# Strassen feed-forward: convolution borders on ScalarE, the convolution in one stretch, weight splits in pairs, another order on VectorE, token sums without GpSimd

## The chip, the cores and the metric

One core of one Trainium2 chip runs the whole program. The metric is the time of one execution in device microseconds (us), the median over several runs. Engines are named PE (TensorE, matrix products), ACT (ScalarE), DVE (VectorE), POOL (GpSimd) and SP (SyncE, which here only issues DMAs).

## The reference, cut to what matters

The program is one step of an encoder trunk of two layers for two groups of requests with shared weights: a prompt of 16 meta tokens and 512 frames, and 8 sample streams of 16 frames. In each layer a token mixer (attention and a gated recurrence) is followed by a gated feed-forward with a causal convolution of width 3. The change is in the feed-forward, and in its two ends.

```
h = rmsnorm(x, p['norm_ffn_pre'])
u = h @ p['w_ffn_up']                                   # 1024 -> 2 x 2816
a, v = u[..., :D_FF], u[..., D_FF:]
ext = concatenate([buf, a], axis=1)                     # 2 earlier rows ahead of each stream
c = ffn_conv_b + sum(ext[:, j:j + T] * w[j] for j in range(3))
f = (silu(c) * v) @ p['w_ffn_down']                     # 2816 -> 1024
x = x + rmsnorm(f, p['norm_ffn_post'])
new_buf = ext[:, -2:]
```

## The kernel before, in words

**Layout.** Everything is held as features x tokens: 128 features on the partitions, 656 tokens on the free axis (528 of the prompt, then 8 x 16 of the samples). A matrix product works on halves of 328 tokens. Weights and activations are in float32 and are multiplied in three products: each operand is split into a rounded high part and the remainder as the low part. ACT writes the high part (`whi`, `gh`, `Hh`, `Sh`), DVE subtracts it from the original for the low part (`wlo`, `gl`, `Hl`, `Sl`). One 128x128 weight block so costs three matmuls of 128x328 for each half. The helpers that record an instruction give all of an engine's the same line: 768 for PE, 2100 for DVE, 1453 for ACT; the tiles' names tell them apart.

**Up projection.** The 2816 features are 22 chunks of 128 (`KF`), each with an `a` part and a `v` part. The first three (`NPL`) are plain: six tiles, weight pieces P_UP to P_UP+5. Chunks 3 to 21 are computed by Strassen's seven products in the order B11, B21, T2, T3, T1, T4, B22. Each needs a split weight of 128x512 (a *unit*): B11, B21 and B22 are quarters of the loaded pieces, T1 to T4 are sums of them. GpSimd forms the sums by DMAs that add in memory, one after another: `sum_t3`, `sum_t4`, then `sum_t1` and `sum_t2` of the next chunk (lines 725, 733, 711, 719). Each waits for the one before it; T2 lies in `t2` (two buffers), T3 in `t3` (one), and T3's own start is loaded by SP when the last chunk's T3 has been split. T4 is written over B21, and so waits for the split of B21. The products go to banks of `G0`/`G1` and of `WA`. The token side of the products is `Hh`/`Hl` and the sums `Sh`/`Sl`, made once per layer: GpSimd's `token_sums` writes two differences into `Y`, ACT and DVE scale and add them there, `s_high` and `s_low` split them.

**What follows a chunk.** DVE adds products into `ax` (`a`, first half of the tokens after B21, the second after T4, by way of the buffers `p1`, `p7` and `u2`, which ACT fills by copies). The names in the convolution: `halo(c)` copies the two earlier rows of each sample stream from `cout` into `ax`, `carry(c)` copies the last two rows of `a` into `cout`, both on DVE. `conv_first` (ACT) is the first tap with the bias, `conv_rest` (DVE) the other two, each in two pieces: 528 prompt tokens and 8 x 16 sample tokens. `silu` and `g_high` are ACT's, `times_v` and `g_low` DVE's. The convolution of a chunk (the *pending* one) is done while the next chunk's products run.

**Down projection.** The chunks are in groups (0 to 1, 2 to 5, 6 to 9, 10 to 13, 14 to 17, 18 to 21). After each group TensorE multiplies its 4 chunks into 8 output tiles n = 0 to 7 (three banks of PSUM in rotation), and DVE adds them to `Y`; after the first group ACT copies them.

**What sets the order.** Every engine's instructions are written out by hand, with semaphores. Split units stand in a ring of six half slots. `split_after` gives for each unit the place in ACT's and DVE's order at which it is split: when the unit whose slot it takes has been used, later by `LATE` units of its kind. `chunk(c, pending)` calls `lows(l, u)` (DVE) and `highs(l, u)` (ACT), which issue the splits due up to unit `u`.

```
LATE = {B11: 0, B21: 0, T2: 2, T3: 1, T1: 1, T4: 1, B22: 0}
...
            if _k and product_of(_w):
                _w += LATE[_k[1]]
            _i = max(_i, _w)
            split_after.setdefault(_i, []).append(_u)
```

## Time and profile before

| | |
|---|---|
| time, median of 3 runs (range) | 1988.31 us (1988.12 to 1990.95) |
| profiled execution: time, span of its core | 1987.89 us, 1986.1 us |
| granted clock of TensorE, mean | 0.985 |
| PE busy | 1825.2 us (92%) |
| PE weight loads busy | 1658.3 us (83%) |
| DVE busy | 1313.5 us (66%), 2229 instructions |
| ACT busy | 962.6 us (48%), 1601 instructions |
| POOL busy | 242.9 us (12%) |
| chain of waits that ended last | PE 58%, DVE 21%, ACT 10%, DMA 5%, issue 4% |

The profile is of one execution. A row of the views gives a start and a duration in us, the engine, the program's line, and output and input tiles; what stands in brackets is the engine's idle time just before and what ended it. The chain of waits is followed back from the last instruction, at each step to what released it. The granted clock is TensorE's, as a share of its full speed.

### The profile page before, as it was taken

The numbers are of one execution on the slowest core, as the hardware profiler recorded it, in microseconds if no ns is written. First come the engines' busy times: TensorE is split into PE (matmuls) and PEld (weight loads), VectorE is DVE, ScalarE is ACT, GpSimd is POOL, SyncE is SP. The second block draws the span as 40 slices with busy tenths as digits, with TensorE's granted clock in tenths as the row PEclk, the third lists the DMA queues.
The fourth block names the chain that finished last, engine by engine and source line by source line (L and its number), as shares of the span: only waits on it lengthen the run. The fifth ranks groups of instructions, "written<-read, shape, count | busy, mean of one in ns | idle before, by whom it ended". The sixth has DMA issues, their size and how long they took to land.

```text
span 1986.1 us, 31514 instructions
## 1 busy us (share of the span) xinstructions
PE 1825.2 (92%) x11636; PEld 1658.3 (83%) x11636; DVE 1313.5 (66%) x2229; ACT 962.6 (48%) x1601; POOL 242.9 (12%) x261
## 2 busy tenths in 40 slices
...
GB/s 189 72 55 66 68 89 46 131 54 49 152 123 138 144 145 131 133 154 123 43 107 55 52 72 80 63 118 68 65 84 132 133 131 150 131 140 150 139 69 59
DMA packets 98713, 203.71 MB, mean 103 GB/s; under 512 B 16800, under 2 KB 35616, under 8 KB 98536
## 3 DMA queue, kind: packets, MB, share of 16 engines
...
HBM read 170.65 MB, written 8.65 MB: 90 GB/s over the span
## 4 chain that ended last, share of the span: by engine, by line
PE 58%; DVE 21%; ACT 10%; DMA 5%; issue 4%; DVEq 0%; POOL 0%; ACTq 0%; SPq 0%; POOLq 0%
PE G L768 36%; PE WA L768 12%; PE WB L768 8%; DVE tmp L2100 6%; DVE wlo L2100 4%; ACT tmp L1453 3%; DMA t<-in_wstream 3%; DVE ax L2100 2%; DVE Y L2100 2%; DMA wraw<-in_wstream 1%; PE G L772 1%; ACT sq L1453 1%; DVE gl L2100 1%; ACT Y L1453 1%; PE WB L772 1%
## 5 line engine op out<-in xcount | busy, mean ns | idle before, releaser
L768 PE MATMUL G<-Hh,wlo 128*128 128x328 f32 x1384 | 456.8, 330 | 56.5 <-DVE p L2100 32.5
L768 PE MATMUL G<-Hh,whi 128*128 128x328 f32 x1384 | 436.8, 316 | 0.0
L768 PE MATMUL G<-Hl,whi 128*128 128x328 f32 x1384 | 435.8, 315 | 0.0
L768 PEld LDWEIGHTS G<-Hh,wlo 128*128 128x128 f32 x1384 | 264.3, 191 | 76.5 <-DVE p L2100 40.2
L768 PEld LDWEIGHTS G<-Hh,whi 128*128 128x128 f32 x1384 | 264.6, 191 | 2.3 <-issue 0.4
L768 PEld LDWEIGHTS G<-Hl,whi 128*128 128x128 f32 x1384 | 263.8, 191 | 0.0
L1453 ACT ACTIVATE whi<-wraw 128x1024 fp32r<-128x1024 f32 (+2 forms) x194 | 160.3, 826 | 184.2 <-PE G L768 113.2
L2100 DVE TENSOR_TENSOR wlo<-wraw,whi 128x1024 fp32r<-128x1024 f32 (+2 forms) x194 | 181.7, 936 | 45.1 <-ACT whi L1453 28.2
L768 PE MATMUL G<-gh,wlo 128*128 128x328 f32 x424 | 136.1, 321 | 23.5 <-DVE tmp L2100 17.1
L2100 DVE SCALAR_TENSOR_TENSOR tmp<-ax,cols,tmp 128x528 f32<-128x528 f32 (+1 forms) x176 | 98.6, 560 | 57.9 <-ACT tmp L1453 51.8
L768 PE MATMUL G<-gh,whi 128*128 128x328 f32 x424 | 134.5, 317 | 0.0
L768 PE MATMUL G<-gl,whi 128*128 128x328 f32 x424 | 133.3, 314 | 0.0
L768 PE MATMUL G<-Sh,wlo 128*128 128x328 f32 x304 | 97.2, 320 | 25.8 <-DVE wlo L2100 25.8
L2100 DVE TENSOR_TENSOR wlo<-wff,whi 128x512 fp32r<-128x512 f32 (+1 forms) x118 | 91.3, 774 | 27.3 <-ACT whi L1453 16.3
L1453 ACT ACTIVATE whi<-wff 128x512 fp32r<-128x512 f32 (+1 forms) x118 | 82.6, 700 | 50.5 <-PE WB L768 33.0
L768 PEld LDWEIGHTS G<-gh,wlo 128*128 128x128 f32 x424 | 81.1, 191 | 28.0 <-DVE tmp L2100 20.4
L1453 ACT ACTIVATE tmp<-ax,cols 128x528 f32<-128x528 f32 x88 | 58.3, 662 | 88.1 <-DVE cout L2100 85.8
L768 PE MATMUL G<-Sl,whi 128*128 128x328 f32 x304 | 95.0, 313 | 0.0
L1453 ACT ACTIVATE whi<-t 128x512 fp32r<-128x512 f32 x76 | 48.2, 635 | 96.0 <-PE G L768 53.1
L768 PE MATMUL G<-Sh,whi 128*128 128x328 f32 x304 | 94.5, 311 | 0.0
L768 PE MATMUL WA<-Hh,wlo 128*128 128x328 f32 x216 | 70.6, 327 | 20.7 <-ACT p L1453 20.7
L768 PEld LDWEIGHTS G<-Sh,wlo 128*128 128x128 f32 x304 | 57.2, 188 | 32.4 <-issue 32.4
...
## 6 DMA issues: line engine op xcount, KB each, us to landing
...
t<-in_wstream SPq DMA_DIRECT2D x76, 256.0 KB, 4.1
t<-in_wstream POOLq DMA_DIRECT2D x38, 256.0 KB, 5.5
...
wff<-in_wstream POOLq DMA_DIRECT2D x20, 256.0 KB, 4.2
t<-wff POOLq DMA_DIRECT2D x20, 256.0 KB, 3.3
wff<-t POOLq DMA_DIRECT2D x20, 256.0 KB, 3.3
```

The costliest lines, as they stand in the source:

```text
L768: return pe.matmul(out, lhsT, rhs, start=start, stop=stop, skip_group_check=True)
L772: return pe.transpose(out, in_, ident[0:n, 0:n])
L1453: return act.activation(*args, **kw)
L2100: return kind(*args, **kw)
```

## The change

What it does, part by part.

- **Pairs.** Where two units that follow one another lie side by side in the ring and are due together, they are split by one instruction of 1024 columns, not two of 512 (`pair_of`, `w_high_two`, `w_low_two`). `t2` and `t3` become one tile `t23` so that T2 and T3 can be a pair. The due places are set anew by `LATE`.
- **Convolution.** ACT does `halo` and `carry`. The convolution goes into a buffer of its own, `cc`, in one stretch of 672 columns (prompt, and samples with the columns between them), so two instructions on DVE for four and one on ACT for two; `silu` takes the result from `cc` in two pieces. `cc` lies over `cos4`, so that `cos4` is loaded anew in layer 1 (four DMAs on SP).
- **Order.** DVE's `chunk` takes the low parts ahead of the convolution and the pairs at other places; ACT's copies `p7` after `g_high`. Where the feed-forward starts, the plain chunks, weight splits and sums stand in another order.
- **Token sums.** `token_sums` goes from GpSimd. The sums are formed by DVE from `X` (`s_sum`) in `Sf`, `gh_f` and `gl_f`, which lie over `Sh`, `gh` and `gl`; three of the splits into `Sh` and `Hh` now stand in the first down pass, on ACT behind the copy of `Y` for n = 3.
- **Ends.** Behind the last down pass the additions for tiles 3 and 4 stand further back, ACT's table load and the splits of the next layer's first weights further ahead.

The diff, cut to what the text speaks of (the ends are as the last point says):

```diff
-LATE = {B11: 0, B21: 0, T2: 2, T3: 1, T1: 1, T4: 1, B22: 0}
+LATE = {B11: 1, B21: 0, T2: 1, T3: 0, T1: 0, T4: 1, B22: 0}
+PAIRS = (B11, T2, T4)
...
-if not l:
-    sp.dma_start(cos4[32 * i:32 * i + 32, :], a["rope"][64:96, :]).then_inc(S("cos_in"), 16)
+sp.dma_start(cos4[32 * i:32 * i + 32, :], a["rope"][64:96, :]).then_inc(S("cos_in"), 16)
...
-def token_sums(l):
-    pool.wait_ge(S("hl"), (l + 1) * SPLITS)
-    a_, b_ = cols_of(0), cols_of(1)
-    pool.tensor_tensor(Y[:, 0:KH, a_], X[:, 0:KH, a_], X[:, 0:KH, b_], ALU.subtract).then_inc(S("d"), 1)
-    pool.tensor_tensor(Y[:, KH:KD, a_], X[:, KH:KD, b_], X[:, KH:KD, a_], ALU.subtract).then_inc(S("d"), 1)
...
+def pair_of(g):
+    k = product_of(g % UNITS_L)
+    return k is not None and k[1] in PAIRS and ring[g + 1] == ring[g] + 1 and \
+        any(g % UNITS_L in v and g % UNITS_L + 1 in v for v in split_after.values())
...
+def w_high_two(l, u):
...
+act.wait_ge(S(unit_end(w)[0]), unit_end(w)[1])
...
-w_high(l, v)
+if pair_of(l * UNITS_L + v):
+    w_high_two(l, v)
+elif not pair_of(l * UNITS_L + v - 1):
+    w_high(l, v)
...
+def halo(c):
+    step(f(samples(ax[:, c % 2, 2 + PT:EXT], DT + 2)[:, :, 0:2],
+           cout[:, c, 2:2 + DB * 2].rearrange("p (b t) -> p b t", t=2), ACT.Copy))
 def conv_first(c):
-    k = l * KF + c
-    act.wait_ge(S("conv"), 2 * k + 1)
+    act.wait_ge(S("ax"), l * KF + c + 1)
+    did(f(cc[:, 0:EXT - 2], ax[:, c % 2, 0:EXT - 2], ACT.Identity, scale=cols[:, l, C_CW + c:C_CW + c + 1],
+          bias=cols[:, l, C_CB + c:C_CB + c + 1]), "silu")
+def carry(c):
+    step(f(cout[:, c, :].rearrange("p (b t) -> p b t", t=2),
+           samples(ax[:, c % 2, PT - DT:EXT], DT + 2)[:, :, DT:DT + 2], ACT.Copy))
+def silu(c):
+    act.wait_ge(S("conv"), l * KF + c + 1)
+    k, d = l * KF + c, tmp[:, c % 2, :]
     if k >= 2:
         act.wait_ge(S("gl"), 2 * k - 2)
-    s_, d = ax[:, c % 2, :], tmp[:, c % 2, :]
-    kw = dict(scale=cols[:, l, C_CW + c:C_CW + c + 1], bias=cols[:, l, C_CB + c:C_CB + c + 1])
-    step(f(d[:, 0:PT], s_[:, 0:PT], ACT.Identity, **kw))
-    did(f(samples(d[:, PT:T]), samples(s_[:, 2 + PT:EXT], DT + 2)[:, :, 0:DT], ACT.Identity, **kw), "silu")
-def silu(c):
-    act.wait_ge(S("conv"), 2 * (l * KF + c) + 2)
-    did(f(tmp[:, c % 2, :], tmp[:, c % 2, :], ACT.Silu), "silu")
...
+w_high(l, P_UP + 4)
 for k in range(KH):
...
+halo(0)
 conv_first(0)
-act.wait_ge(S("d"), 2 * l + 1)
-for k in range(KH):
-    did(f(Y[:, k, cols_of(0)], Y[:, k, cols_of(0)], ACT.Copy, scale=cols[:, l, C_FFNPRE + k:C_FFNPRE + k + 1]), "s_act")
+halo(1)
+carry(0)
+w_high(l, P_UP + 5)
 silu(0)
-w_high(l, P_UP + 4)
+conv_first(1)
+carry(1)
 g_high(0)
-w_high(l, P_UP + 5)
-conv_first(1)
-s_high(Sh[:, 1, :, :], 4, 0, 1, -1.0)
 silu(1)
 w_high(l, P_UP + 6)
 g_high(1)
-s_high(Sh[:, 2, :, :], 0, 0, 0)
+halo(2)
+conv_first(2)
+carry(2)
+s_high(Sh[:, 1, :, :], Sf[:, 1, :, :], 8, -1.0)
+s_high(Sh[:, 2, :, :], Sf[:, 2, :, :], 4)
+silu(2)
 w_high(l, P_UP + 7)
...
 conv_first(pending)
+carry(pending)
...
+halo(c)
 highs(l, u0 + B21)
 after(T2)
 did(f(u2, bank(G[s], 0), ACT.Copy), "act_took")
 highs(l, u0 + T2)
+if pending is not None:
+    g_high(pending)
 after(T3)
 act.wait_ge(S("gl"), 2 * (l * KF + c) - 1)
 did(f(p7[:, :], bank(WA, s), ACT.Copy), "act_took")
-if pending is not None:
-    g_high(pending)
-highs(l, u0 + T3)
...
-    s_high(Hh[:, 0:KH, cols_of(1)], 8, 1, 0)
 g_high(last_c)
 for n in range(KD):
     if not q:
         act.wait_ge(S("down"), down_no(l, q, n))
-        act.wait_ge(S("s_dve"), s_split(l, 1 if n < KH else 3))
         did(f(two(Y[:, n, :]), halves(down_bank(n)), ACT.Copy), "act_took")
+    if not q and n == 3:
+        s_high(Sh[:, 0, :, :], Sf[:, 0, :, :], 18)
+        act.wait_ge(S("tile"), t0 + T_UP + 2 * NPL)
+        for x in range(2):
+            s_high(Hh[:, 2 * x:2 * x + 2, cols_of(1)], s4_part(x), 12, -1.0)
...
+def w_low_two(l, u):
+    g = l * UNITS_L + u
+    dve.wait_ge(S("w_hi"), g + 2)
+    did(tt_(pair_in(wlo, g), raw_pair(g), pair_in(whi, g), ALU.subtract), "w_split", by=2)
...
 def conv_rest(c):
     dve.wait_ge(S("silu"), 2 * (l * KF + c) + 1)
-    s_, d = ax[:, c % 2, :], tmp[:, c % 2, :]
-    sv, dv = samples(s_[:, 2 + PT:EXT], DT + 2), samples(d[:, PT:T])
+    n_ = EXT - 2
     for i in (1, 2):
-        w = col(l, C_CW + i * KF + c)
-        step(stt(d[:, 0:PT], s_[:, i:i + PT], w, d[:, 0:PT], ALU.mult, ALU.add))
-        did(stt(dv, sv[:, :, i:i + DT], w, dv, ALU.mult, ALU.add), "conv" if i == 2 else "dve")
...
+def s_sum(to, k, x, minus, plus=False):
+    did(stt(to, X[:, k, cols_of(x)], col(l, C_FFNPRE + k), minus, ALU.mult, ALU.add if plus else ALU.subtract),
+        "s_dve")
...
 plain_a(0)
+plain_a(1)
+w_low(l, P_UP + 4)
 conv_rest(0)
-dve.wait_ge(S("s_act"), 2 * KH * l + KH)
+dve.wait_ge(S("s_act"), S_ACT * l + KH)
 for k in range(KH):
...
 plain_v(1)
+plain_a(2)
 w_low(l, P_UP + 6)
 g_low(1)
+conv_rest(2)
+plain_v(2)
+w_low(l, P_UP + 7)
...
+    s_sum(s4_part(k // 2)[:, k % 2, :], KH + k, 0, Sf[:, 1, k, :])
+s_low(0, Sl[:, 1, :, :], Sf[:, 1, :, :], Sh[:, 1, :, :], -1.0)
+s_low(1, Sl[:, 2, :, :], Sf[:, 2, :, :], Sh[:, 2, :, :])
...
+lows(l, u0 - 2)
 if pending is not None:
     conv_rest(pending)
-lows(l, u0 - 2)
-halo(c)
-lows(l, u0 - 1)
+lows(l, u0 + B11)
 after(B21)
 dve.wait_ge(S("act_took"), act_took(l, c, 0))
-did(tt_(s_[:, 2:2 + HALF], bank(G[s], 1), p1, ALU.add), "dve")
+step(tt_(s_[:, 2:2 + HALF], bank(G[s], 1), p1, ALU.add))
 step(tt_(s_[:, 2:2 + HALF], s_[:, 2:2 + HALF], R[:, cols_of(0)], ALU.mult))
-lows(l, u0 + B11)
 if pending is not None:
     times_v(pending)
-lows(l, u0 + B21)
+lows(l, u0 + T2)
 if pending is not None:
     g_low(pending)
-lows(l, u0 + T2)
 after(T1)
 dve.wait_ge(S("act_took"), act_took(l, c, 2))
 did(tt_(p7[:, :], p7[:, :], bank(G[s], 0), ALU.add), "dve_took")
-lows(l, u0 + T3)
+lows(l, u0 + T1)
 after(T4)
 step(tt_(u2, u2, bank(WA, s), ALU.add))
 sv = samples(s_[:, 2 + PT:EXT], DT + 2)
 step(tt_(s_[:, 2 + HALF:2 + PT], u2[:, 0:PT - HALF], R[:, HALF:PT], ALU.mult))
-step(tt_(sv[:, :, 2:], samples(u2[:, PT - HALF:HALF]), samples(R[:, PT:T]), ALU.mult))
-carry(c)
-lows(l, u0 + T1)
+did(tt_(sv[:, :, 2:], samples(u2[:, PT - HALF:HALF]), samples(R[:, PT:T]), ALU.mult), "ax")
...
-s_low(3, Hl[:, 0:KH, cols_of(1)], Hh[:, 0:KH, cols_of(1)], 1, 0)
+for k in range(KH):
+    s_sum(Sf[:, 0, k, :], KH + k, 1, Sf[:, 0, k, :])
+s_low(2, Sl[:, 0, :, :], Sf[:, 0, :, :], Sh[:, 0, :, :])
+for x in range(2):
+    s_low(3 + x, Hl[:, 2 * x:2 * x + 2, cols_of(1)], s4_part(x),
+          Hh[:, 2 * x:2 * x + 2, cols_of(1)], -1.0)
```

DVE, from the last additions of chunk 3 (the first Strassen chunk of group (2, 6)) to the first ones of chunk 4. `t2` and `t3` are T2's and T3's weight sums, `p7`, `R2` (which holds `u2`) and `ax` take the products, `cout` holds the rows that are carried. Before:

```order
L2100 TENSOR_TENSOR p7<-p7,G1 128x328 [waits w_split,act_took,product]
L2100 TENSOR_TENSOR R2<-R2,WA 128x328 [waits dve_took,product]
L2100 TENSOR_TENSOR ax<-R2,R 128x200 [waits dve]
L2100 TENSOR_TENSOR ax<-R2,R 128x8x16 [waits dve]
L2100 COPY cout<-ax 128x18 [waits dve]
L2100 SCALAR_TENSOR_TENSOR tmp<-ax,cols,tmp 128x528 [waits conv,silu]
L2100 SCALAR_TENSOR_TENSOR tmp<-ax,cols,tmp 128x128 [waits dve]
L2100 SCALAR_TENSOR_TENSOR tmp<-ax,cols,tmp 128x528 [waits dve]
L2100 SCALAR_TENSOR_TENSOR tmp<-ax,cols,tmp 128x128 [waits dve]
L2100 TENSOR_TENSOR wlo<-t2,whi 128x512 [waits conv,w_hi]
L2100 TENSOR_TENSOR wlo<-t3,whi 128x512 [waits w_split,w_hi]
L2100 COPY ax<-cout 128x8x2 [waits w_split]
```

And of the change (`t23` holds `t2` and `t3`, `cc` the convolution):

```order
L2158 TENSOR_TENSOR p7<-p7,G1 128x328 [waits w_split,act_took,product]
L2158 TENSOR_TENSOR wlo<-t23,whi 128x1024 [waits dve_took,w_hi]
L2158 TENSOR_TENSOR R2<-R2,WA 128x328 [waits w_split,product]
L2158 TENSOR_TENSOR ax<-R2,R 128x200 [waits dve]
L2158 TENSOR_TENSOR ax<-R2,R 128x8x16 [waits dve]
L2158 TENSOR_TENSOR wlo<-wraw,whi 128x512 [waits ax,w_hi]
L2158 SCALAR_TENSOR_TENSOR cc<-ax,cols,cc 128x672 [waits w_split,silu]
L2158 SCALAR_TENSOR_TENSOR cc<-ax,cols,cc 128x672 [waits dve]
L2158 TENSOR_TENSOR wlo<-wraw,whi 128x1024 [waits conv,w_hi]
L2158 TENSOR_TENSOR ax<-G0,R2 128x328 [waits w_split,act_took,product]
```

The split of T2 and T3 has moved from behind the convolution to just behind the addition into `p7`, as one instruction of 1024 columns; the copy into `cout` is gone, and the convolution is two instructions.

ACT, in the first down pass, whose tiles it copies to `Y` (`Hh` is the high part of the token features, `gh` that of the gated chunk). Before:

```order
L1453 ACTIVATE Hh<-Y 128x4x328 [waits w_hi,s_dve,tile]
L1453 ACTIVATE gh<-tmp 128x656 [waits s_act,gl]
L1453 ACTIVATE Y<-G0 128x656 [waits gh,s_dve,down]
L1453 ACTIVATE Y<-WB 128x656 [waits act_took,s_dve,down]
L1453 ACTIVATE Y<-G1 128x656 [waits act_took,s_dve,down]
L1453 ACTIVATE Y<-G0 128x656 [waits act_took,s_dve,down]
L1453 ACTIVATE whi<-t2 128x512 [waits act_took,down,T]
L1453 ACTIVATE whi<-t3 128x512 [waits w_hi,down,T3]
L1453 ACTIVATE Y<-WB 128x656 [waits w_hi,s_dve,down]
L1453 ACTIVATE Y<-G1 128x656 [waits act_took,s_dve,down]
```

And of the change:

```order
L1480 ACTIVATE gh<-tmp 128x656 [waits w_hi,gl]
L1480 ACTIVATE Y<-G0 128x656 [waits gh,down]
L1480 ACTIVATE Y<-WB 128x656 [waits act_took,down]
L1480 ACTIVATE Y<-G1 128x656 [waits act_took,down]
L1480 ACTIVATE Y<-G0 128x656 [waits act_took,down]
L1480 ACTIVATE Sh<-Sf 128x1312 [waits act_took,s_dve]
L1480 ACTIVATE Hh<-gh_f 128x2x328 [waits s_act,s_dve,tile]
L1480 ACTIVATE Hh<-gl_f 128x2x328 [waits s_act,s_dve]
L1480 ACTIVATE whi<-t23 128x1024 [waits T3,down,s_act,T]
L1480 ACTIVATE Y<-WB 128x656 [waits w_hi,down]
L1480 ACTIVATE Y<-G1 128x656 [waits act_took,down]
L1480 ACTIVATE Y<-G0 128x656 [waits act_took,down]
```

The split into `Hh` has moved from ahead of all copies to between the fourth and the fifth copy, with one into `Sh` ahead of it, which waits for DVE's sums by `s_dve`.

## Rows read from the trace of the kernel before

**Rows 1.** Waits of TensorE, 537:954: who, for what: idle us, times, longest.

```profile
PE G L768 <- DVE p L2100: 16.5, 14, 1.6
PE G L768 <- DVE wlo L2100: 13.2, 14, 2.1
PE WA L768 <- ACT p L1453: 10.3, 14, 1.4
```

**Rows 2.** Chain of waits, whole execution: start, us, what.

```profile
587.36 3.87 PE G L768 x24
...
691.56 7.20 PE G L768 x48
...
953.63 3.90 PE G L768 x24
```

**Rows 3.** Timeline of PE where layer 0's feed-forward starts.

```profile
494.98 0.61 PE L768 MATMUL G<-Hh,wlo 128*128 128x328 f32 x1 [4.00 <-DVE wlo L2100]
...
520.90 0.64 PE L768 MATMUL G<-gh,wlo 128*128 128x328 f32 x1 [3.54 <-DVE tmp L2100]
...
535.61 0.31 PE L768 MATMUL G<-Hh,wlo 128*128 128x328 f32 x1
```

**Rows 4.** Timeline of DVE: start, us, instruction, idle before and releaser.

```profile
623.14 0.17 DVE L2100 COPY cout<-ax 128x18 f32<-128x18 f32 x1
624.73 2.35 DVE L2100 SCALAR_TENSOR_TENSOR tmp<-ax,cols,tmp 128x528 f32<-128x528 f32 x4 [1.43 <-ACT tmp L1453]
627.19 1.49 DVE L2100 TENSOR_TENSOR wlo<-t,whi 128x512 fp32r<-128x512 f32 x2
```

**Rows 5.** Timeline of ACT: the same columns.

```profile
623.34 1.36 ACT L1453 ACTIVATE tmp<-ax,cols 128x528 f32<-128x528 f32 x2 [2.59 <-DVE cout L2100]
...
639.69 0.64 ACT L1453 ACTIVATE whi<-t 128x512 fp32r<-128x512 f32 x1 [3.93 <-DMA t<-in_wstream]
```

**Rows 6.** Windows: us, PE, PEld, DVE, ACT, POOL, clock, DMA, GB/s.

```profile
495.00:498.00 3.00, 3.00 (x11) 3.00 (x12) 2.65 (x7) 0.90 (x2) 0.00 (x0) 0.50 0.55 168
```

**Rows 7.** Groups by form, DVE and ACT: busy us, mean ns, idle before.

```profile
L2100 DVE TENSOR_TENSOR wlo<-wraw,whi 128x1024 fp32r<-128x1024 f32 x92 | 113.2, 1230 | 34.5 <-ACT whi L1453 27.4 <-DVEq L2100 0.6
...
L2100 DVE SCALAR_TENSOR_TENSOR tmp<-ax,cols,tmp 128x528 f32<-128x528 f32 x88 | 67.6, 769 | 54.8 <-ACT tmp L1453 51.8
...
L2100 DVE SCALAR_TENSOR_TENSOR tmp<-ax,cols,tmp 128x128 f32<-128x128 f32 x88 | 31.0, 352 | 3.1
...
L1453 ACT ACTIVATE whi<-wraw 128x1024 fp32r<-128x1024 f32 x92 | 97.5, 1060 | 93.0 <-PE G L768 77.2 <-DMA wraw<-in_wstream 3.3 <-DMA o_conv<-cout 2.0
...
L1453 ACT ACTIVATE tmp<-ax,cols 128x528 f32<-128x528 f32 x44 | 36.5, 830 | 86.6 <-DVE cout L2100 85.8
...
L1453 ACT ACTIVATE tmp<-tmp 128x656 f32<-128x656 f32 x44 | 33.1, 753 | 17.5 <-DVE tmp L2100 14.5 <-ACT whi L1453 0.4
```

**Rows 8.** Timeline of POOL: the issues of sums T1 and T2.

```profile
641.43 0.87 POOL L711 DMA_DIRECT2D wff<-in_wstream  x1 [3.60 <-DMA wraw<-t]
645.67 0.86 POOL L719 DMA_DIRECT2D t<-wff  x1 [3.37 <-DMA wff<-in_wstream]
```

**Rows 9.** Timeline of POOL: a T2 sum issued late, and the T3 sum.

```profile
593.01 0.86 POOL L719 DMA_DIRECT2D t<-wraw  x1 [5.28 <-DMA wraw<-in_wstream]
593.54 1.22 POOL L725 DMA_DIRECT2D t<-in_wstream  x1
```

**Rows 10.** DMA issues: KB each, median us from issue to landing.

```profile
t<-in_wstream POOLq DMA_DIRECT2D x38, 256.0 KB, 5.5
```

**Rows 11.** Timeline of POOL: the second token sum.

```profile
480.65 4.01 POOL L698 TENSOR_TENSOR Y<-X 128x1312 f32<-128x1312 f32 x1
```

**Rows 12.** Timeline of DVE: a copy beside it.

```profile
482.76 1.94 DVE L2100 COPY ax<-cout 128x16 f32<-128x16 f32 x1
```

**Rows 13.** Timeline of DVE: the first residual multiplication behind layer 0.

```profile
976.65 0.50 DVE L2100 TENSOR_TENSOR tmp<-Y,R 128x328 f32<-128x328 f32 x1 [1.10 <-ACT R L1453]
```

**Rows 14.** Chain of waits: a load of T3.

```profile
1876.48 7.48 DMA t<-in_wstream
```

More of the change, by code:

```diff
@@ L214, in build @@
         ff = ExitStack()
+        gw = ExitStack()
+        gh_f = sb(gw, "gh_f", [P, G4, T])
+        gl_f = sb(gw, "gl_f", [P, G4, T])
+        gw.close()
         gh = sb(ff, "gh", [P, G4, T], F32R)
@@ L753, in _ @@
                 split_out(l, range(HG))
-                token_sums(l)
                 sum_t1(l, NPL)
@@ L1438, in _, with did @@
             count, last = {}, []
-            def did(ins, name, at=None):
-                count[name] = at or count.get(name, 0) + 1
+            def did(ins, name, at=None, by=1):
+                count[name] = at or count.get(name, 0) + by
                 last[:] = [name]
-                ins.then_inc(S(name), 1)
+                ins.then_inc(S(name), by)
             def prev():
@@ L1539, in _ @@
             split_to = [0]
+            def w_high_two(l, u):
+                g = l * UNITS_L + u
+                for v in (g, g + 1):
+                    act.wait_ge(S(raw_ready(v)[0]), raw_ready(v)[1])
+                    for w in users[v]:
+                        act.wait_ge(S(unit_end(w)[0]), unit_end(w)[1])
+                did(f(pair_in(whi, g), raw_pair(g), ACT.Copy), "w_hi", by=2)
             def highs(l, u):
@@ L1950, in _ @@
                         conv_first(last_c)
+                        carry(last_c)
                         highs(l, u0 - 1)
@@ L1991, in ffn_out_b @@
                     did(f(sq[:, c % 2, cols_of(1)], Y[:, n, cols_of(1)], ACT.Square), "sq")
-                for n in (3, 4):
-                    ffn_out_b(n)
-                    scale_y(n, 1)
                 def high(x, k):
@@ L2021, in _ @@
                     square(0, 1)
-                    w_high(l + 1, 0)
-                    ffn_out_b(KD - 3)
+                    ffn_out_b(3)
+                    w_high(l + 1, 1)
+                    scale_y(3, 1)
                     high(0, 2)
                     high(0, 3)
+                    ffn_out_b(4)
+                    scale_y(4, 1)
+                    ffn_out_b(KD - 3)
                     scale_y(KD - 3, 1)
-                    w_high(l + 1, 1)
+                    w_high(l + 1, 2)
                     ffn_out_b(KD - 2)
-                    w_high(l + 1, 2)
                     scale_y(KD - 2, 1)
```

138 lines of the change are left out of this document (73 added, 65 removed).

## The prediction, on record before the changed kernel ran

> **What bounds the kernel now.** TensorE's queue is the same, row for row, before and after the change, so the change can win only time in which TensorE waits or runs at its lower clock. I read first what TensorE waits for, then the chain of waits, then the queues that it waits for. In layer 0's stretch of Strassen chunks TensorE waits 40.0 us for three things [rows 1]: a weight's low part (DVE `wlo`), the addition into `p7` (DVE) and the copy of `p7` (ACT), 14 times each, once per chunk that is not the first of its group. None is a missing transfer. The chain gives the scale: 48 products of 128x328 take 7.20 us, 0.150 each. A group of four chunks and its down pass has 4 x 84 + 192 = 528 of them, 79.2 us. Four groups of layer 0 took 953.63 - 587.36 = 366.3 us for 316.8 [rows 2]: 49.5 lost. The first group, from its first product at 535.61 [rows 3] to 587.36, took 51.8 for 43.2 (three chunks and 5.4 of the down pass): 8.6 lost. I take layer 1 alike: in all 116 us lost with the chunks.
>
> Why, in one chunk: the convolution on DVE starts late, since it waits for ACT, whose first tap waits for DVE's `carry`; the low parts of T2 and T3 stand behind the convolution [rows 4], and TensorE waits for them. ACT in turn stands 3.93 us for T3's sum [rows 5], whose load starts only when the last T3 is split.
>
> Ahead of the chunks each layer has a second loss. Tile P_UP+4 waits 4.00 us for a weight split that stands behind the convolution and the token sums, and two more waits follow, the longer 3.54 us [rows 3]. After such a gap the granted clock reads 0.50 (1.2 GHz) [rows 6], and 11 products take 3.00 us, 0.27 each. Up to 535.61 that is 16.0 us in layer 0.
>
> **The change, part by part.** Durations are those of the profiled execution (1987.89 us; the median is 0.4 above).
>
> *Pairs.* DVE's low part of 512 columns costs 0.69 (two with their gap 1.49 [rows 4]), of 1024 it costs 1.23 [rows 7]: 0.26 saved by a pair. ACT's 0.64 [rows 5] twice with a gap 0.1 against 1.06 [rows 7]: 0.32. The order has 90 pairs for 38 chunks, 2.4 each (the ring's end breaks the rest): DVE -0.6, ACT -0.75 per chunk.
>
> *Convolution in one stretch.* From 0.769 at 528 and 0.352 at 128 columns [rows 7] DVE pays 0.22 and 1.04 ns a column: 0.92 for 672, twice 1.88 against 2.35 [rows 4], -0.5. ACT's first tap: 0.83 at 528 [rows 7]; 672 lies between that and 1.06 (in proportion), I take 0.95, nearer the smaller since part of it is fixed; against 1.36 for its two pieces [rows 5], -0.4. SiLU becomes two pieces: 0.75 [rows 7] becomes about 1.03, as ACT's fixed part is 0.22 (from 0.64 and 1.06), +0.3.
>
> *Borders on ACT.* DVE gives up two copies of 0.17 [rows 4] with gaps, -0.5; ACT takes two of about 0.24 with gaps, +0.7 (bounds 0.35 and 0.9). The Trainium skill speaks against this move (VectorE: DVE Perf Modes, the section on the TRN2 errata): a fixed 224 cycles at 1.2 GHz per ScalarE instruction, 187 ns, but 58 at 0.96 GHz, 60 ns, on VectorE. By these DVE would give up only 0.15 and ACT take 0.4 for it, a loss on the pair of engines. The trace has 172 ns for DVE's 18 columns [rows 4], not 79, so here both engines pay much the same and the move is nearly neutral in work.
>
> Sum per chunk: DVE -1.6; the pieces left, walked below, fill 11.8 of TensorE's 12.6; ACT about -0.2.
>
> *Order, a chunk walked.* 0 is the start of B11 in a chunk with a pending one, products 1.8 each. DVE: the last `ax` piece until 0.45, T1 low 1.25, convolution 1.7 to 3.6, pair T4/B22 low 4.95 (its high part starts behind the p1 copy, 2.5), first half of `a` 6.15, `times_v` 7.3, pair B11/B21 low 8.65, `g_low` 9.6, `p7` added 10.2; TensorE wants that at 10.8. ACT copies `p7` at 8.3 to 8.75; TensorE wants it at 9.0. T2/T3, low by 11.7, are wanted at 16.2. So all three waits [rows 1] close, with 0.2 to 0.6 us to spare.
>
> But then T3's sum must have landed. POOL's chain runs on from T4's sum, which may start when B21 is split, 8.9: 4.4 to T1's sum (0.87 and 3.60), 4.2 to T2's [rows 8], 0.6 to T3's [rows 9], 5.5 to its landing [rows 10]: 23.6, which is 11.0 in the next chunk, where ACT wanted it at 9.3. What is late then is not T2 but what is queued behind on ACT and DVE: T1's high part, then the `u2` addition, `ax`, the first tap and the p1 copy. The chunk after loses about 0.5 at T2 and 1.1 at T4. This meets one chunk of four (the first has the down pass to work ahead in, the third is itself stretched). With 0.4 more for the others, and 0.9 where the down pass's third tile waits for the last `times_v`, I walk to 2.9 us per group. As the margins above are thin I take 4.5; for the last group, where DVE also multiplies by R, 6.8; for the first, 3.7. That is 3.7 + 3 x 4.5 + 6.8 = 24.0 per layer, 48 of 116: **-68 us**.
>
> *Start of the feed-forward.* POOL's token sums go. While its second ran, 480.65 to 484.66 [rows 11], DVE's 16-column copy took 1.94 in place of 0.17 and ended with it [rows 12]. The Trainium skill (SBUF — State Buffer, "Who interferes with whom") says that GpSimd and such a VectorE copy lock each other out for a whole instruction; the trace agrees, so both the copy's wait and the POOL work fall away. Now `w_high(P_UP+4)` comes first on ACT (482.6 to 483.7), DVE splits it by 486.7, and TensorE needs it at 490.8: the 4.0 wait is gone. Tiles +4 and +5 then end at 505.2. The down pass waits for `plain_v(2)` until 508.5, 1.5 us for the present two waits. DVE then goes through w_low(P_UP+7), four s4 sums, two Sl, one pair and four Sf sums (1.3 + 2.4 + 3.1 + 1.3 + 2.4) until 519.4. ACT, after copying Y3 at 514.8, stands for that count of `s_dve`, does Sh and two Hh until 522.5 and the T2/T3 pair until 523.7, and only then copies Y4, without which TensorE cannot start n=7: it stands from 519.3 to 524.6, 5.3 us, and pays about 1.3 for the lower clock. **A new wait, longer than the one removed.** Chunk 3 starts at 527.7 for 535.6: -7.9, twice, **-16 us**.
>
> *Tails.* `ffn_out_b(3)` and `(4)` no longer stand before R: DVE's residuals begin at 973.7 for 976.65 [rows 13], but take over three to four 0.6 us pieces. -2.3 at layer 0's end; at the kernel's -1.7, with the table load (1.28) moved ahead. **-4 us.** `w_low(l+1, 0)` moves ahead of them, one 1.23 us piece off that chain, in this figure. The reload of cos in layer 1 (four transfers more on SP, ahead of the next weight pieces) is layer 0's own set of eight again: 0, or 1 us at most if a piece is late.
>
> Sum: 1987.9 - 68 - 16 - 4 = **1900 us**. The forecast's own range, from 2.9 to 7 us per group, is 1887 to 1920.
>
> **Rivals.**
> - *All handovers hold*: only 0.9 per down pass and 4.6 in the two last groups remain, 13.6 of 116. 1987.9 - 102.4 - 20 = 1865. For it: the three margins are positive. Against: POOL's chain.
> - *POOL's sums or a full DVE pace every chunk*: 2.5 us lost in each of 28 non-first chunks and the 13.6: 83.6 left, -32.4 - 20, so 1935. For it: DVE has 0.8 us free of 12.6.
> - *The start wins nothing* (the Y4 wait grows by 8 us, the sums being later still): 1916.
> - *Slower*: ACT, standing for a late T3 sum, now holds T1's high part, the first tap and the p1 copy behind it. With the slow steps that occur now and then (T1 to T2 6.1 [rows 9], T3 7.5 to land [rows 14]) T3 comes 4.4 + 6.1 + 0.6 + 7.5 after 8.9, 14.9 us into the next chunk; p1 is then copied at 20.6 for 16.2, 4.4 lost, and 1.1 at T4 as above: 5.5 in each of 28 chunks, 154 + 13.6 for 116, +52 - 20, so 2019. It decides from 4.4 us per chunk, (116 + 20 - 13.6) / 28. Against: both steps are exceptions.
> - *No effect*: DVE's queue was not what held TensorE, the waits go back to the chain of sums: 1988.
>
> **Chances.** Forecast 0.55, all hold 0.10, paced 0.20, start alone 0.07, slower 0.05, no effect 0.03. The range takes in the paced case and half the way to the best: 1880 to 1940. A measurement of this kernel tells about 0.2% (4 us) from no change. Faster 0.92, same 0.03, slower 0.05.
>
> **What would show it.** Right: four-chunk groups of 84 us; no wait for `wlo` at tile P_UP+4; TensorE waiting some 5 us for Y before n=7 of the first down pass, with the clock at 0.5 after; ACT still waiting for T3's sum in the second chunk of a group. DVE busy some 46 us less (90 x 0.15, 88 x 0.20 and 88 x 0.17). Wrong: waits of over 2 us for `p7` or `wlo` in every chunk, or a group over 88 us.

## The result and the profile after

The changed kernel takes 1934.38 us (median of 4 runs, 1932.28 to 1937.73), the kernel before 1989.63 in the same comparison: ratio 0.9723, 95% interval 0.9711 to 0.9735. It is faster, by 55 us and not by the 88 that were forecast; the time lies in the stated range. The profiled execution took 1932.28 us.

First the page's busy times, then its shares of the chain of waits:

```profile
PE 1820.8 (94%) x11636; PEld 1668.9 (86%) x11636; DVE 1267.4 (66%) x1973; ACT 951.0 (49%) x1593; POOL 229.5 (12%) x257
...
PE 56%; DVE 17%; DMA 13%; ACT 9%; issue 3%; DVEq 0%; POOL 0%; ACTq 0%; SPq 0%; POOLq 0%
```

DVE is busy 46.1 us less, as forecast (46). But the share of DMA in the chain has gone from 5% to 13%: something that was hidden now leads. What TensorE waits for, over the whole execution (us in total, times, longest):

```profile
PE G L795 <- ACT R L1480: 34.2, 12, 4.2
PE WB L795 <- ACT Y L1480: 9.8, 2, 4.9
PE G L795 <- DVE tmp L2158: 9.3, 11, 2.6
...
PE WA L795 <- ACT p L1480: 6.1, 10, 1.2
PE G L795 <- DVE wlo L2158: 2.7, 2, 1.9
```

The three waits of [rows 1] are nearly gone: the one for DVE's `p` stands no more in the view. In their place TensorE waits 12 times, 34.2 us, for ACT's copy into R2 (the tile `R` of the view): the copy of p1, without which T2 cannot start. The second line is the new wait of the first down pass, once in each layer.

The marks of [rows 2, 3] in the changed kernel: the start of chunk 3 in both layers (timeline of PE), and the third tile of the down passes (chain of waits).

```profile
527.34 0.47 PE L795 MATMUL G<-Hh,wlo 128*128 128x328 f32 x1
...
1475.75 0.48 PE L795 MATMUL G<-Hh,wlo 128*128 128x328 f32 x1
```

```profile
574.32 3.87 PE G L795 x24
...
924.88 3.88 PE G L795 x24
...
1523.80 3.88 PE G L795 x24
...
1870.66 3.89 PE G L795 x24
```

And layer 1 of the kernel before, which stood in no group (timeline of PE, chain of waits):

```profile
1509.11 0.31 PE L768 MATMUL G<-Hh,wlo 128*128 128x328 f32 x1
```

```profile
1559.83 3.87 PE G L768 x24
...
1927.09 3.88 PE G L768 x24
```

| stretch | before | after | difference | forecast |
|---|---|---|---|---|
| to chunk 3, layer 0 | 535.61 | 527.34 | -8.3 | -7.9 |
| first group, layers 0 and 1 | 51.75, 50.72 | 46.98, 48.05 | -7.4 | |
| four groups, layers 0 and 1 | 366.27, 367.26 | 350.56, 346.86 | -36.1 | all chunks: -68 |
| end of layer 0 to chunk 3 of layer 1 | 555.48 | 550.87 | -4.6 | -10.2 |
| end of the kernel | 59.0 | 59.8 | +0.8 | -1.7 |

The forecast missed the profiled time by 32 us. 24 of them are in the chunks, 5.6 between the layers, 2.5 at the end. Over their 79.2 us of products the six groups between the first and the last of a layer lost 6.3 to 8.3 us, 7.1 in the mean, where 2.9 were walked and 4.5 taken; the last ones lost 11.2 and 9.8 for 6.8. The first group of layer 0 lost 3.8, as walked (3.7), that of layer 1 4.9. By the prediction's own sign of being wrong, a group over 88 us, the last groups (90.4 and 89.0) are over the line and the six others (85.5 to 87.5) are not.

One late chunk, followed back from TensorE's wait at 629.79 (chain of waits, 606 to 630 us; start, us, what):

```profile
606.79 3.26 DMA wff<-t
...
610.60 3.71 DMA wraw<-in_wstream
...
615.38 8.63 DMA t<-in_wstream
...
624.25 1.07 ACT whi L1480
...
625.40 1.24 DVE wlo L2158
...
627.99 0.96 ACT cc L1480
...
629.30 0.45 ACT R L1480
```

TensorE's own row there (timeline of PE):

```profile
629.79 0.42 PE L795 MATMUL G<-Sh,wlo 128*128 128x328 f32 x1 [2.92 <-ACT R L1480]
```

GpSimd's adding DMAs (T4, T1, then T3 beside T2) end when T3 lands at 624.0. ACT has then stood for it, and behind it come the pair's high part, its low part on DVE, the additions into `ax` and the first tap, and only then p1's copy: 5.8 us from T3's landing to TensorE. T3's DMA took 8.63 us; the page gives a median of 6.5 for its kind, where [rows 10] had 5.5:

```profile
t<-in_wstream POOLq DMA_DIRECT2D x38, 256.0 KB, 6.5
```

It did not run alone. The timelines of POOL and of SP's queue, then the windows of 9 us (the columns of [rows 6]):

```profile
614.84 0.86 POOL L747 DMA_DIRECT2D t<-wraw  x1 [3.38 <-DMA wraw<-in_wstream]
615.38 1.22 POOL L753 DMA_DIRECT2D t<-in_wstream  x1
620.87 0.86 POOL L761 DMA_DIRECT2D wraw<-t  x1 [4.27 <-DMA t<-wraw]
```

```profile
615.43 0.81 SPq L652 DMA_DIRECT2D wff<-in_wstream  x2
616.27 0.45 SPq L610 DMA_DIRECT2D t<-in_wstream  x1
```

```profile
606.00:615.00 9.00, 9.00 (x62) 9.00 (x61) 6.74 (x10) 5.14 (x8) 1.88 (x3) 1.00 0.47 94
615.00:624.00 9.00, 9.00 (x61) 9.00 (x61) 4.96 (x8) 3.11 (x6) 2.46 (x3) 1.00 0.90 226
```

SP issues the next weights 0.05 us behind T3's sum (two loads of 512 KB and one of 256), T2's sum is under way, and the DMA engines are busy 0.90 of the time T3 needs, for 0.47 before. The T3 sums ahead of the 12 waits took 6.9 to 9.8 us, 8.3 in the median. From T4's issue to the next one, 606.79 to 620.87, the sums take 14.1 us, and a chunk of products 12.6.

Two things in GpSimd's queue have changed with it. In the kernel before 27 of the 38 T3 sums waited for T3's own load (55.0 us in all) and so started apart from T2's; now that T3 is split earlier 9 do (11.8 us), and 27 start within 0.6 us of T2's. These take 6.9 us in the median, ten others 4.2. The neighbour alone does not explain it: in the kernel before those close to T2's took 5.8 and the others 5.5. And T4's sum, which in the kernel before always waited for B21's split, now waits 13 times for T2's sum (waits of POOL):

```profile
POOL wraw L761 <- DMA t<-wraw: 44.0, 8, 6.4
POOL wff L761 <- DMA t<-wff: 19.8, 5, 4.1
```

In the chunk above T2's sum took 5.5 us from issue to landing, for a median of 3.3 in the kernel before.

### The profile page after: what moved, and what is told of

The parts are those of the page before. It is cut to its first block, busy times and chain, and to the rows that moved or that the text cites. A ratio compares the mean times of both kernels' runs of the same rounds, so it can differ in the third digit from the quotient of the medians.

```text
span 1930.5 us, 31256 instructions
## 1 busy us (share of the span) xinstructions
PE 1820.8 (94%) x11636; PEld 1668.9 (86%) x11636; DVE 1267.4 (66%) x1973; ACT 951.0 (49%) x1593; POOL 229.5 (12%) x257
## 3 DMA queue, kind: packets, MB, share of 16 engines
q0 software_dynamic: 21888, 39.86, 12.6%
## 4 chain that ended last, share of the span: by engine, by line
PE 56%; DVE 17%; DMA 13%; ACT 9%; issue 3%; DVEq 0%; POOL 0%; ACTq 0%; SPq 0%; POOLq 0%
PE G L795 34%; PE WA L795 11%; PE WB L795 8%; DVE wlo L2158 5%; DMA t<-in_wstream 4%; DMA wraw<-in_wstream 2%; ACT whi L1480 2%; DMA t<-wraw 2%; DVE tmp L2158 2%; DMA wff<-in_wstream 2%; DVE cc L2158 1%; DMA wraw<-t 1%; DMA wff<-t 1%; PE G L799 1%; DVE ax L2158 1%
## 5 line engine op out<-in xcount | busy, mean ns | idle before, releaser
L795 PE MATMUL G<-Hh,wlo 128*128 128x328 f32 x1384 | 452.4, 327 | 11.8 <-DVE Hl L2158 8.0
L1480 ACT ACTIVATE whi<-wraw 128x1024 fp32r<-128x1024 f32 (+2 forms) x171 | 155.6, 910 | 187.0 <-PE G L795 114.7
L2158 DVE TENSOR_TENSOR wlo<-wraw,whi 128x1024 fp32r<-128x1024 f32 (+2 forms) x171 | 177.6, 1038 | 54.4 <-ACT whi L1480 41.8
L795 PE MATMUL G<-Sh,wlo 128*128 128x328 f32 x304 | 100.9, 332 | 34.2 <-ACT R L1480 34.2
L2158 DVE TENSOR_TENSOR wlo<-wff,whi 128x1024 fp32r<-128x1024 f32 (+1 forms) x85 | 86.0, 1012 | 36.1 <-ACT whi L1480 30.9
L1480 ACT ACTIVATE whi<-t 128x1024 fp32r<-128x1024 f32 (+1 forms) x42 | 41.1, 979 | 134.9 <-PE G L795 69.7
L1480 ACT ACTIVATE whi<-wff 128x1024 fp32r<-128x1024 f32 (+1 forms) x85 | 75.7, 891 | 47.4 <-PE WB L795 33.0
L795 PE MATMUL G<-Sh,whi 128*128 128x328 f32 x304 | 98.9, 325 | 0.0
L2158 DVE TENSOR_TENSOR wlo<-t,whi 128x1024 fp32r<-128x1024 f32 (+1 forms) x42 | 47.2, 1124 | 72.6 <-ACT whi L1480 71.6
L2158 DVE SCALAR_TENSOR_TENSOR cc<-ax,cols,cc 128x672 f32<-128x672 f32 x88 | 80.9, 919 | 18.3 <-ACT cc L1480 16.2
L795 PEld LDWEIGHTS G<-gh,wlo 128*128 128x128 f32 x424 | 79.8, 188 | 13.9 <-DVE tmp L2158 12.6
L795 PE MATMUL WB<-gh,wlo 128*128 128x328 f32 x248 | 79.8, 322 | 9.8 <-ACT Y L1480 9.8
```

Source lines behind the costliest of these rows:

```text
L795: return pe.matmul(out, lhsT, rhs, start=start, stop=stop, skip_group_check=True)
L1480: return act.activation(*args, **kw)
L2158: return kind(*args, **kw)
```

## The experiments

The first leaves out the second term of T3; the others compute what the reference asks. Theory A is that the late landing of T3, passed on by the order on ACT and DVE to p1's copy, is what the chunks still lose; B, that DVE and ACT set the pace. Each kernel was compared with the kernel before on the same chip; the changed kernel's 0.9723 is what the ratios are to be held against.

**1. Without T3's adding DMA.** GpSimd's `sum_t3` is not called, ACT waits for T3's first load alone.

```diff
 def raw_ready(g):
     l, u = divmod(g, UNITS_L)
+    if product_of(u) and product_of(u)[1] == T3:
+        return "t3_in", 16 * (chunk_no(l, product_of(u)[0]) + 1)
...
-    sum_t3(l, c)
     sum_t4(l, c)
```

> The changed kernel without GpSimd's adding DMA for T3 (T3 is then only its first term; that part of the feed-forward's product is left out). Theory A, the chain of sums: in the changed kernel GpSimd's four adding DMAs take 14.1 us a chunk for 12.6 of products, T3 lands up to 5 us after ACT wants it, and ACT, standing for it, holds the copy of p1, for which TensorE waits (34.2 us in 12 waits). Then those waits go here: 1890 to 1905 us for the 1934 of the changed kernel. Theory B, the pace of DVE and ACT (each chunk's splits, convolution and copies fill them): the waits only move to wlo, p7 or the copies, 1928 to 1938 us.

1901.98 us, ratio 0.9563 (0.9542 to 0.9584). The waits of TensorE for the two copies:

```profile
PE WA L796 <- ACT p L1481: 11.1, 16, 1.4
PE G L796 <- ACT R L1481: 7.9, 7, 1.9
```

26 of the 34 us for R2 are gone, those for p7 have grown by 5. A holds: T3's sum is the cause of most of it. This run takes the whole transfer away, and so cannot tell T3's own landing from what its sum does to the chain and to the other transfers; the next ones leave the transfers alone.

**2. Low parts behind `ax`.**

```diff
     did(tt_(p7[:, :], p7[:, :], bank(G[s], 0), ALU.add), "dve_took")
-    lows(l, u0 + T1)
     after(T4)
...
     did(tt_(sv[:, :, 2:], samples(u2[:, PT - HALF:HALF]), samples(R[:, PT:T]), ALU.mult), "ax")
+    lows(l, u0 + T1)
```

> The changed kernel with DVE's low parts of the T2/T3 pair moved from ahead of the last three additions into ax to behind them. Theory A: T3's landing stays late, but ax no longer waits for it, so the first tap and the copy of p1 come about 2 us sooner in each of 12 late chunks: 1910 to 1918 us. Theory B: DVE does the same work, 1931 to 1938 us, and slower if the low parts of T2, now 1.2 us later, become the wait.

1915.56 us, 0.9632 (0.9611 to 0.9653): A's value. No work and no DMA has changed, only who stands behind whom:

```profile
PE G L795 <- ACT R L1480: 15.3, 12, 2.9
PE WA L795 <- ACT p L1480: 15.2, 16, 2.0
```

There are 12 waits for R2 again, at less than half. The copy of p7 is late now: DVE's convolution still starts behind the late pair, `times_v` after it, and ACT's `g_high`, behind which the copy stands, waits for that.

**3. The pair behind the first tap too.** On ACT `highs(l, u0 + T1)` and `highs(l, u0 + T4)` leave the chunk's end, on DVE `lows(l, u0 + T1)` and the two `lows(l, u0 - 2)`; the next calls take the splits up, behind tap and convolution.

> The changed kernel with the pair T2/T3 and T1 split behind the pending chunk's first tap and carry on ACT, and behind the rest of its convolution on DVE. Theory A: in a late chunk all that is left is p1 behind the pair, some 0.2 to 0.5 us instead of 2.9: 1903 to 1915 us. A rival inside A: the low part of T2 is then ready only when TensorE wants it (16.1 for 16.2 us after the start of B11), in every chunk, so that the wait passes to wlo, up to 1 us in each of 38 chunks: 1925 to 1945 us. Theory B: 1931 to 1940 us.

1923.32 us, 0.9669 (0.9651 to 0.9688). The waits are those of the rival inside A, the time lies 2 us under its range: R2 is waited for once, and DVE's two are larger (2.7 and 9.3 in the changed kernel):

```profile
PE G L795 <- DVE tmp L2156: 13.1, 10, 3.1
PE G L795 <- DVE wlo L2156: 8.9, 24, 1.9
...
PE G L795 <- ACT R L1480: 0.7, 1, 0.7
```

T2's low part has no slack that far back; that T3, wanted a product later, has it is what run 11 tries. But this edit did something else too. In each layer, ahead of the down pass behind the first group of Strassen chunks, TensorE waits 3.8 us (7.5 in all), for which the view names no releaser. The first low part of that pass, which DVE had done by 567.1 in the changed kernel, stands behind the convolution here and starts at 569.67; TensorE starts at 571.00. That is more than the 6 us by which the waits for `wlo` grew, and about as much as this run is slower than run 2.

**4. Copies of Y first.** In the first down pass:

```diff
-if not q and n == 3:
+if not q and n == 5:
     s_high(Sh[:, 0, :, :], Sf[:, 0, :, :], 18)
...
     s_sum(Sf[:, 0, k, :], KH + k, 1, Sf[:, 0, k, :])
+lows(l, u0 + nk // 2 - 1)
 s_low(2, Sl[:, 0, :, :], Sf[:, 0, :, :], Sh[:, 0, :, :])
```

> The changed kernel with ACT's three splits into Sh and Hh in the first down pass behind the copy of Y for n = 5 and not n = 3, and DVE's low parts of T2/T3 ahead of Sl. Theory A: the wait of 4.9 us for Y and the lower clock behind it go, in both layers, and nothing else is late: chunk 3 starts 6.7 us sooner, 1919 to 1924 us. Rival: another input of chunk 3 (B11's bank, T2's low part, the T4 sum) takes its place, 1930 to 1935 us.

1924.30 us, 0.9679 (0.9661 to 0.9697), 10 us less than the changed kernel (9 by the ratios), just above A's range. The wait for Y is gone; of the 6.7 us per layer 1.75 came back at chunk 3's T2 (timeline of PE), whose first product is at 526.41 for 531.20:

```profile
526.41 0.39 PE L795 MATMUL G<-Sh,wlo 128*128 128x328 f32 x1 [1.75 <-issue]
```

**5. Both edits, and T3's sum ahead of T2's.** The edits of 2 and 4, and on GpSimd:

```diff
+sum_t3(l, NPL)
 for c in range(NPL, KF):
-    sum_t3(l, c)
     sum_t4(l, c)
     if c + 1 < KF:
         sum_t1(l, c + 1)
+        sum_t3(l, c + 1)
         sum_t2(l, c + 1)
```

> The changed kernel with the edits of the two runs before (low parts behind ax; copies of Y first) and GpSimd's adding DMA for T3 issued between those for T1 and T2, not behind T2's. Theory A: the first two edits add up (their gains were 19 and 10 us), which gives 1905; the third edit lets T3 land 2 to 3 us sooner in late chunks, where 0.8 to 1.3 us are still lost at T2 and 1 us at T4, worth 5 to 15 us: 1890 to 1900 us. Theory B for the third edit: T3's load blocks T2's sum when it is late, and the chain gets longer: 1905 to 1915 us.

1913.39 us, 0.9614 (0.9595 to 0.9633), hardly under the second run alone. The timeline of POOL in a late chunk:

```profile
610.54 0.87 POOL L753 DMA_DIRECT2D t<-in_wstream  x1 [3.98 <-DMA t<-in_wstream]
611.08 1.23 POOL L747 DMA_DIRECT2D t<-wraw  x1
620.39 0.86 POOL L761 DMA_DIRECT2D wraw<-t  x1 [8.08 <-DMA t<-wraw]
```

T3 goes out 4.8 us behind T1's sum and 0.5 before T2's, and now it is T2's sum that is long, 8.8 us to its landing. The pair needs both. That is B's value for this edit, and B's cause is seen too: T3's sum has waited for T3's own load (3.98 us in the first row), and T2's stands behind it. The expected 5 to 15 us did not come, and part of the fourth run's gain was given back.

**6. No pairs.** `PAIRS = ()`.

> The changed kernel with every pair split as two units of 512 columns, in the same order. DVE then has 0.6 us more work in a chunk and ACT 0.75. Theory A (late chunks are set by T3's landing, the others have 0.2 to 0.6 us to spare): about half of that is seen in 38 chunks, 1940 to 1958 us. Theory B (DVE's pace sets the chunk): all of it, 1957 to 1965 us.

1924.74 us, 0.9669 (0.9653 to 0.9685): faster than with pairs, below both expectations, though DVE is 14 us busier (1281.6). The timeline of ACT in a late chunk says why:

```profile
619.51 0.63 ACT L1480 ACTIVATE whi<-t 128x512 fp32r<-128x512 f32 x1 [1.50 <-DMA t<-wraw]
622.04 0.63 ACT L1480 ACTIVATE whi<-t 128x512 fp32r<-128x512 f32 x1 [1.90 <-DMA t<-in_wstream]
```

T2 is split when its sum is there, 2.5 us ahead of T3, and behind T3's landing stand 512 columns, not 1024, on either engine. Neither theory had this; both had counted a pair as less work and nothing else.

**7. Borders back on DVE.** `halo` and `carry` as in the kernel before, all else as changed.

> The changed kernel with halo and carry back on DVE, all else kept. In the traces a border costs 0.22 us on ACT and 0.17 on DVE. Theory A: neutral, since what is late is set by T3's landing, though the first tap now waits for DVE's carry, 0.2 us, in each late chunk: 1932 to 1940 us. Theory B, DVE is the fuller engine: 0.4 us more in each of 38 chunks, 1943 to 1950 us.

1935.89 us, 0.9720 (0.9701 to 0.9740), the changed kernel's own value: neutral, as expected by A. In the changed kernel the copies of `carry` are these (those of `halo` take 218 ns)

```profile
L1480 ACT ACTIVATE cout<-ax 128x18 f32<-128x18 f32 x44 | 9.6, 219 | 1.4
```

Here ACT's busy time falls by 19.3 us and DVE's rises by 15.3 (88 copies of 174 ns). By the table in the Trainium skill (VectorE: DVE Perf Modes, the section on the TRN2 errata) an ACT instruction has a fixed part of 224 cycles at 1.2 GHz and a DVE one of 58 at 0.96, by estimate 187 and 60 ns, and 202 and 79 with 18 columns; ACT's 219 ns come near, DVE's 172 to 174 do not.

**8. The order of before.**

```diff
-LATE = {B11: 1, B21: 0, T2: 1, T3: 0, T1: 0, T4: 1, B22: 0}
+LATE = {B11: 0, B21: 0, T2: 2, T3: 1, T1: 1, T4: 1, B22: 0}
```

with DVE's low parts and ACT's `g_high` in `chunk` where they stood.

> The changed kernel with LATE and the order of a chunk (DVE's low parts, ACT's g_high) as before the change; pairs where that order allows them (179 of 1024 columns in place of 202), the convolution in one stretch, the borders on ACT, the start and the sums as changed. Theory A: the order carries most of what the chunks gained (44 us), since T2's low part stands behind the convolution again: 1950 to 1970 us. Rival: the shorter work carries it, 1932 to 1945 us.

1943.03 us, 0.9757 (0.9737 to 0.9777). The rival was right: the new order is worth 0.3% (about 7 us, with intervals that just miss each other), not most of the chunks' 44. It is the order with its pairs: the old one allows 179 instructions of 1024 columns for 202, as many of them for T2 and T3. The waits have the names of [rows 1] again:

```profile
PE G L795 <- DVE wlo L2159: 27.5, 22, 4.2
PE G L795 <- DVE p L2159: 22.3, 23, 1.6
```

In the one late chunk that was followed back (TensorE waits 2.15 us at 630.18) T3 lands at 624.4, and its low part comes behind it and the convolution. There either order loses to a late T3, the old one at `wlo`, the new one at p1's copy; how much of the two waits above is this was not told apart. GpSimd's queue has gone back too: 21 of the T3 sums wait for T3's own load again (36.7 us), and T4's sum waits for T2's only twice (9.6 us). So it is the new order that brought the sums together, and part of what it won it paid for there.

**9. T2 alone.** `PAIRS = (B11, T4)`.

> The changed kernel with T2 and T3 split as two units of 512 columns and the other pairs kept. Theory A: what cost time in the run without pairs was the pair T2/T3 alone: it ties T2's split, whose sum has landed, to T3's landing, and makes ACT and DVE do 1024 columns, not 512, after it (1.06 for 0.63 us and 1.23 for 0.69). The other pairs only save work. Then this is at least as fast as without pairs (1925): 1917 to 1926 us. Rival: the pair B11/B21 costs it, since B21's split, for which T4's sum waits, comes later in a pair: then 1931 to 1938 us here.

1920.58 us, 0.9646 (0.9616 to 0.9675), its runs 1913.79 to 1926.47. The pair T2/T3 alone was what cost; by how much the other pairs help is not told at this spread.

**10. T2 alone, and the edits of 2 and 4.**

> As the run before, with the two edits that gained singly: DVE's low part of T2 and T3 behind the additions into ax, and the copies of Y first. Theory A: three different waits, so the gains add up but for the late chunks, where low parts behind ax and T2 alone shorten the same wait: 1898 to 1908 us. Rival: POOL's chain of sums sets the late chunks whatever the order, as in the combination with the other order of sums (1913): 1910 to 1915 us.

1897.73 us, 0.9542 (0.9523 to 0.9562): the lower end of A's range. The gains add up, which with the pair T2/T3 and the other order of sums (run 5) they had not.

**11. T3 behind the first tap.** As 10, and

```diff
-LATE = {B11: 1, B21: 0, T2: 1, T3: 0, T1: 0, T4: 1, B22: 0}
+LATE = {B11: 1, B21: 0, T2: 1, T3: 1, T1: 0, T4: 1, B22: 0}
...
     highs(l, u0 + T1)
-    highs(l, u0 + T4)
...
-    lows(l, u0 - 2)
     if pending is not None:
         conv_rest(pending)
...
-    lows(l, u0 - 2)
     if q:
         conv_rest(last_c)
```

> As the run before, and T3 (with T1) split behind the pending chunk's first tap and carry on ACT and behind the rest of its convolution on DVE; T2 stays ahead of them. Theory A: ACT now stands for T3's landing with only T1 and the copy of p1 behind it, and T3 is wanted 1.8 us later than T2, so a late T3 costs at most its own lateness: the waits of TensorE for R2 fall under 0.5 us a late chunk and those for p7 with them: 1885 to 1898 us. Rival: with less waiting the sums come closer together and land later still, or the down pass waits for the last times_v, later by T3's and T1's splits: 1900 to 1912 us.

1890.87 us (1885.42 to 1894.09), 0.9505 (0.948 to 0.953): A's value. The waits for p7 and R2 in its profile:

```profile
PE WA L795 <- ACT p L1480: 12.5, 20, 1.3
...
PE G L795 <- ACT R L1480: 3.4, 6, 1.9
```

R2 has gone from 34.2 to 3.4 us (10.6 in run 10); p7's waits have not followed (12.9 in run 10), against the expectation. The intervals of 10 and 11 touch.

**12. The ends as before.** As 11, with ACT's and DVE's instructions behind the last down passes in the order before the change.

> The run before (T3 behind the first tap) with the two ends behind the last down passes put back to the order before the change, on ACT and DVE. In the changed kernel the stretch from the last down pass's third tile (TensorE's wait for times_v) to the norm's sum took 42.35 us at layer 0's end for 41.17 before, and 59.8 to the end of the span for 59.0. Theory A, the new order of the ends is what costs it: 41.2 and 59.0 again, 1888 to 1890 us. Rival, as the prediction had it, the new order gains and something else costs: both stretches longer than in the changed kernel, 43.5 or more and 61, 1893 to 1896 us. A difference under 2 us is told by the stretches of the profile, not by the medians.

1887.17 us (1885.70 to 1889.41), 0.9485 (0.9465 to 0.9504): the intervals of 11 and 12 overlap. The stretches are 42.70 us at layer 0's end (run 11: 42.35) and 61.2 at the kernel's (59.5), where A wanted 41.2 and 59.0; the one behind it, from the norm's sum of layer 0's output to that ahead of layer 1's feed-forward, is 438.35 (439.75; 438.36 in the kernel before). Neither expectation held by these values, but two of the differences are TensorE's clock. Behind the same wait for `times_v` (2.15 us in both) the clock is down in run 12 (windows of PE; run 11 has 1.00 there):

```profile
899.00:902.00 3.00, 2.92 (x11) 2.93 (x12) 0.86 (x2) 0.75 (x1) 0.00 (x0) 0.50 0.02 5
```

The 24 products of that tile take 5.37 us for 3.88, so that the old order's 42.7 is the 41.2 of before and 1.5 us of clock: A holds for layer 0's end, the new order costs 1.2 us there. The 1.4 us of the stretch behind it are of the same kind: in layer 1's mixer, which no edit touches, 3 us have a granted clock of 0.50 in run 11 and 0.53 in the changed kernel, and of 1.00 in run 12 and before. Why the kernel's end is 61.2 in the order that took 59.0 is open.

The last two are both faster than the kernel before and the changed one by more than their intervals.

## Why the prediction was right, and where it was off

**Direction, range and bound.** Right, the range in part by luck: the forecast's own, 1887 to 1920, was missed by 14 us, and 1934 lies in the stated 1880 to 1940 only since that takes in the "paced" rival, whose cause was not the one at work. TensorE's queue was the same and only waits were won. DVE's relief of 46 us is 46.1; a DVE stretch of 672 columns measured 919 ns for 0.92 worked out, ACT's first tap 950 ns for 0.95:

```profile
L2158 DVE SCALAR_TENSOR_TENSOR cc<-ax,cols,cc 128x672 f32<-128x672 f32 x88 | 80.9, 919 | 18.3 <-ACT cc L1480 16.2
...
L1480 ACT ACTIVATE cc<-ax,cols 128x672 f32<-128x672 f32 x44 | 41.8, 950 | 71.7 <-DVE ax L2158 70.6 <-DVEq L2158 0.8
```

**Start of the feed-forward: -16, measured -15.4** (-8.3 and, from the norm's sum to chunk 3, 75.95 to 68.84 in layer 1, -7.1). The wait of P_UP+4 is gone and the new one stands where it was said to, 4.92 us for 5.3, with a granted clock of 0.50 in the 3.2 us after it, and ACT's own wait behind it:

```profile
518.86 1.30 ACT L1480 ACTIVATE Sh<-Sf 128x1312 fp32r<-128x1312 f32 x1 [4.52 <-DVE Sf L2158]
...
523.12 0.72 ACT L1480 ACTIVATE Y<-WB 128x656 f32<-128x656 f32 x1
```

**Chunks: -68, measured -43.5.** The mechanism was right, and its size was off first in one term of the sum: "5.5 to its landing". The median over 38 DMAs was taken for one that in the late chunks starts together with T2's sum and, in the one shown, with SP's weights; there it took 8.63, 3.1 more. T1's sum came 0.6 sooner than counted (3.8 for 4.4). With these two the walk's 0.5 us at T2 becomes 3.0; TensorE waited 2.92 there. How much of the 3.1 us is T2's sum and how much SP's loads no run shows: none moved the loads. The sentence that this "meets one chunk of four" was the second part of it: in two of layer 0's groups two chunks were late, since the chain of sums (14.1 us for 12.6) falls further behind. For that the walk lacked a wait: it had T4's sum "start when B21 is split", and 13 times it waited for T2's sum. The allowance for thin margins, from 2.9 to 4.5 us per group, would have had to reach 7.1.

**Pairs.** Their saving per instruction was right (1226 and 1060 ns for 1024 columns), their place was not weighed: a pair waits for the later of its two inputs, and what stands behind it then waits for more columns. The prediction priced the T2/T3 pair as -0.26 and -0.32 us; without pairs the kernel was 0.5% faster.

**Borders.** "Nearly neutral in work" held in the time too (run 7). The figures of that table had the move as a loss; by DVE's 172 to 174 ns there is none.

**Order.** It was costed as what lets all three waits close. With T3 late it was worth 0.3%, pairs included (run 8).

**Ends: -4, measured +0.8 at the kernel's end and +2.5 behind layer 0** (-4.6 less the start's -7.1). Most of this is clock: of the 2.5 us, 1.3 are the 3 us at 0.53 in layer 1's mixer (run 12), and at the kernel's end the eight products for the norm took 3.56 us for 2.60, at 0.69 for 0.98. Without them the ends are +1.2, up to the norm's sum, and about -0.1, for a forecast of -2.3 and -1.7. At layer 0's end DVE's residuals did begin sooner (22.1 us behind the mark for 23.0), but TensorE then waited for ACT's square:

```profile
961.51 0.92 PE L795 MATMUL WA<-sq,ones 128*128 128x328 f32 x1 [3.03 <-ACT sq L1480]
```

That square (960.99) stood on ACT behind the square of a tile of Y, for which ACT waited on DVE:

```profile
959.79 0.48 ACT L1480 ACTIVATE sq<-Y 128x328 f32<-128x328 f32 x1 [1.44 <-DVE Y L2158]
```

DVE adds that tile later in the new order. The reload of cos cost nothing that can be seen: with it and the old ends (run 12) the stretch behind the norm is 438.35 us, as before.

**Rivals.** The "slower" rival named the mechanism that ruled (ACT standing for T3 with p1 behind it), at 4.4 us in all 28 chunks; it came in 12, at 0.9 to 4.2. The "paced" rival gave 1935, the very time, by the wrong cause: DVE's pace was not the bound, as the runs without pairs (more work, less time) and with the borders on DVE show. What of the chunks' 44 us each part of the change brought was not told apart beyond the order (gained about 7), the borders (nothing) and the pairs (lost about 10); the convolution in one stretch was not tried alone.
